# Two fused transformer blocks: another order around the two attentions, the out product and the last stores

## The reference, cut to what matters

```python
# block 1
xn = rmsnorm(x, norm_mix_g)
q_lat, kv_lat, k_rope, dq, dk, dv, gate_pre = split(xn @ w_in)
q, kv = rmsnorm(q_lat) @ mla_w_uq, rmsnorm(kv_lat) @ mla_w_ukv        # 8 heads, rope on 32 of 96 columns
o_mla = causal_attention(q_mla, k_mla, v_mla)
o1, o2 = causal_attention(dq[0], dk[0], dv), causal_attention(dq[1], dk[1], dv)   # 4 heads
o_diff = rmsnorm(o1 - lam * o2, diff_subln_g) * (1 - lambda_init)
g_mla, g_diff = split(sigmoid(gate_pre + b_gate))
merged = g_mla * (o_mla @ w_branch_mla) + g_diff * (o_diff @ w_branch_diff)
x = x + merged @ w_out
hn = rmsnorm(x, norm_ffn_g)
x = x + (silu(hn @ w_ffn_gate) * (hn @ w_ffn_up)) @ w_ffn_down
x = rmsnorm(x, norm_final_g)
# block 2
q, k, v, za, u, vs, zs, gm = split(rmsnorm(x, norm_g_2) @ w_in_2)
a = window_sink_attention(rope(q), rope(k), v, sinks)                 # 16 heads, keys of 128 + 64 tokens
a = (a * silu(za)) @ w_att_out
sgo = gelu(u) * (masked(w_s) @ layernorm(gelu(vs)) + b_s)
sgo = (sgo * silu(zs)) @ w_sg_out
ga, gs = split(sigmoid(gm + b_merge))
x = x + (ga * a + gs * sgo) @ w_o
return rmsnorm(x, final_g)
```

## Time and profile before

| | |
|---|---|
| median of 3 runs | 1262.26 us (1262.21 to 1262.78) |
| profiled execution | 1262.92 us, span 1261.2 us |
| TensorE's granted clock, mean | 0.999 |
| busy: PE | 1241.1 us, 98% |
| busy: DVE | 818.7 us, 65% |
| busy: ACT | 558.7 us, 44% |
| busy: POOL | 147.0 us, 12% |
| moved by DMA | 149.03 MB, mean 118 GB/s |

### The profile page before, as it was taken

How to read it: one execution, slowest core, us unless ns; L and a number is a source line. 1 busy time by engine, 2 the same in 40 slices (tenths; PEclk the granted TensorE clock), 3 DMA queues, 4 the chain that set the end, 5 groups by cost and what they waited for, 6 DMA issues and landing times.

```text
span 1261.2 us, 15542 instructions
## 1 busy us (share of the span) xinstructions
PE 1241.1 (98%) x6018; PEld 1039.8 (82%) x6018; DVE 818.7 (65%) x1272; ACT 558.7 (44%) x966; POOL 147.0 (12%) x208
## 2 busy tenths in 40 slices
PE   9999999999999999999999999999999999999997
PEld 8878888888878888888888888878888888888885
DVE  6885667754687555665665579858875436436687
ACT  5456564652455333333332263437763343223344
POOL 0001341231000100100000000005550000000200
PEclk9999999999999999999999999999999999999999
DMA  6242323129564943793332233321105322332971
GB/s 201 67 108 65 84 76 93 51 84 231 186 167 146 254 135 100 224 210 100 100 129 89 91 97 108 122 68 38 63 3 189 111 82 86 102 99 88 234 171 76
DMA packets 119077, 149.03 MB, mean 118 GB/s; under 512 B 14358, under 2 KB 90204, under 8 KB 119004
## 3 DMA queue, kind: packets, MB, share of 16 engines
q1 hardware_dynamic: 105436, 115.53, 28.8%
q0 software_dynamic: 13552, 32.51, 11.9%
q10 hardware_dynamic: 16, 0.00, 0.0%
HBM read 142.78 MB, written 2.10 MB: 115 GB/s over the span
## 4 chain that ended last, share of the span: by engine, by line
PE 86%; DVE 7%; ACT 3%; issue 2%; POOL 1%; DVEq 0%; ACTq 0%; POOLq 0%
PE ps_mm L2454 57%; PE ps_mm L2489 9%; PE ps_s L2757 3%; PE ps_mm L2757 3%; PE ps_t L2757 2%; PE ps_o L2757 2%; DVE w_lo L1513 1%; PE ps_s L2615 1%; ACT w_hi L908 1%; PE ps_o L2646 1%; PE ps_o L2902 1%; PE ps_mm L2529 1%; PE ps_s L2668 1%; PE ps_t L2626 1%; PE ps_o L2695 1%
## 5 line engine op out<-in xcount | busy, mean ns | idle before, releaser
L2454 PE MATMUL ps_mm<-act_hi,w_hi 128*128 128x512 f32 x944 | 372.2, 394 | 1.1 <-DVE w_lo L1513 1.1
L2454 PE MATMUL ps_mm<-act_hi,w_lo 128*128 128x512 f32 x944 | 370.0, 392 | 0.0
L2454 PE MATMUL ps_mm<-act_lo,w_hi 128*128 128x512 f32 x944 | 369.8, 392 | 0.0
L1513 DVE TENSOR_TENSOR w_lo<-stage,w_hi 128x2048 fp32r<-128x2048 f32 (+5 forms) x98 | 205.2, 2094 | 127.8 <-ACT w_hi L908 127.6
L908 ACT ACTIVATE w_hi<-stage 128x2048 fp32r<-128x2048 f32 (+5 forms) x99 | 171.9, 1736 | 143.1 <-PE ps_mm L2454 65.6
L2454 PEld LDWEIGHTS ps_mm<-act_hi,w_hi 128*128 128x128 f32 x944 | 177.4, 188 | 37.2 <-DVE w_lo L1513 2.4
L2454 PEld LDWEIGHTS ps_mm<-act_hi,w_lo 128*128 128x128 f32 x944 | 177.3, 188 | 35.6
L2454 PEld LDWEIGHTS ps_mm<-act_lo,w_hi 128*128 128x128 f32 x944 | 177.4, 188 | 34.7
L2489 PE MATMUL ps_mm<-w_hi,act_hi 128*128 128x512 f32 (+2 forms) x144 | 52.7, 366 | 0.6 <-DVE lat L1643 0.5
L2489 PE MATMUL ps_mm<-w_lo,act_hi 128*128 128x512 f32 (+2 forms) x144 | 52.2, 362 | 0.0
L2489 PE MATMUL ps_mm<-w_hi,act_lo 128*128 128x512 f32 (+2 forms) x144 | 52.2, 362 | 0.0
(11 more groups left out here) (518 smaller groups left out, 2363.4 us busy)
## 6 DMA issues: line engine op xcount, KB each, us to landing
stage<-in_w_in SPq DMA_DIRECT2D x43, 1024.0 KB, 5.3
sums<-in_w_ffn_down POOLq DMA_DIRECT2D x16, 1024.0 KB, 9.4
stage<-in_w_ffn_gate SPq DMA_DIRECT2D x11, 1024.0 KB, 7.6
stage<-in_w_ffn_up SPq DMA_DIRECT2D x11, 1024.0 KB, 7.0
stage<-in_w_ffn_down SPq DMA_DIRECT2D x8, 1024.0 KB, 5.0
osum<-in_w_out POOLq DMA_DIRECT2D x6, 1024.0 KB, 9.3
tsum<-in_w_o POOLq DMA_DIRECT2D x6, 1024.0 KB, 8.4
stage<-in_w_out SPq DMA_DIRECT2D x4, 1024.0 KB, 4.9
```

The source lines that it names most:

```text
L1513: V.tensor_tensor(w_lo[:, s, 0:k * w], raw, w_hi[:, s, 0:k * w].bitcast(F32), ALU.subtract).then_inc(w_lo_made, 1)
L2454: ins = T.matmul(ps_mm[:, 2 * bank_slot + m, :], wt[:, kk, m * P:(m + 1) * P], acts[ap][:, kk, :], start=(r == 0), stop=(r == per - 1), sk ...
```

## The change

In words: the first MLA scores are issued inside `mv` ahead of token block 3 (token order 0, 1, 2, 3); the squares of the last diff head move behind that step's gate banks and `hi`; in the merge ScalarE's sums come ahead of the gate banks and `hi` of the next unit between the two banks, VectorE's lo of the sums between the two gate products; in the stage of out the order of chunks, sums and units' lo changes (chunk 6's lo before chunk 5's) on both engines, and VectorE takes P6 out of its bank before P2; wg is turned one unit earlier, and VectorE's work on it, x3 and the sinks come before the last bank of za; `w_lo` in the window stream is made in quarters over four steps; the output is stored in eight halves.

```diff
@@ orders
+KEPT = {n: ("P6", "P2", "P7", "P5", "P4", "P3") if n == "out" else tuple(q for q in ORDER[n] if q != "P1") for n in GROUPED}
-    return 12 * GROUPED.index(n) + 2 * [q for q in ORDER[n] if q != "P1"].index(p)
+    return 12 * GROUPED.index(n) + 2 * KEPT[n].index(p)
+MERGED_LO = (0, 1, 2, 3, 4, 6, 5, 7)
@@ SP: stores
-            for pos, t in enumerate(FIN_ORDER[:3]):
-                sp.wait_ge(fin_made, pos + 1)
-                sp.wait_ge(fin_made_act, pos + 1)
-                sp.dma_start(ov[:, t, :], res[:, t, :]).then_inc(out_written, 16)
...
+            for half, t in ((0, 2), (1, 2), (1, 3), (0, 3), (0, 0), (1, 0), (0, 1), (1, 1)):
+                made = FIN_ORDER.index(t) + 1
+                sp.wait_ge(fin_made, made) if half else sp.wait_ge(fin_made_act, made)
+                cols = slice(512 * half, 512 * half + 512)
+                sp.dma_start(ov[:, t, cols], res[:, t, cols]).then_inc(out_written, 16)
@@ ScalarE: diff head, merge, out
-                if 0 <= hd < DH and r == 0:
+                if 0 <= hd < DH - 1 and r == 0:
...
                 for u in DIFF_STREAM.started(p):
                     hi(u + 1)
+                if hd == DH - 1 and r == 0:
+                    for t in range(TT):
+                        act.wait_ge(o_copied, 4 * hd + t + 1)
+                        squares(o_sb[:, t * P:(t + 1) * P], o_sq[:, t * P:(t + 1) * P], diff_ssq[:, t:t + 1], o_squared)
...
             for i in range(1, 4):
                 hi(GATE_B[i] + 1)
-                for m in range(2):
-                    gate_bank(GATE_B[i], m, 8 + 2 * i + m)
-                hi(MRG_D[i - 1] + 1)
                 if i > 1:
                     merged_sums_hi(i - 2)
+                gate_bank(GATE_B[i], 0, 8 + 2 * i)
+                if i < 3:
+                    hi(MRG_D[i - 1] + 1)
+                gate_bank(GATE_B[i], 1, 8 + 2 * i + 1)
                 if i < 3:
                     for m in range(2):
                         merge_hi(2 * i - 2 + m)
+                else:
+                    hi(MRG_D[i - 1] + 1)
+            merge_hi(4)
             hi(uo)
-            merge_hi(4)
             merge_hi(5)
+            merged_sums_hi(2)
+            hi(uo + 1)
             merge_hi(6)
-            hi(uo + 1)
             merge_hi(7)
-            merged_sums_hi(2)
@@ VectorE: quarters, merge, out
+            def lo_quarter(u, h):
...
+                n = k * w // 4
+                ins = V.tensor_tensor(w_lo[:, s, h * n:(h + 1) * n], stage[:, s, h * n:(h + 1) * n],
+                                      w_hi[:, s, h * n:(h + 1) * n].bitcast(F32), ALU.subtract)
+                if h == 3:
+                    ins.then_inc(w_lo_made, 1)
...
                 lo(GATE_B[i] + 1)
-                for m in range(2):
-                    gate_norm(GATE_B[i], m, 8 + 2 * i + m)
-                lo(MRG_D[i - 1] + 1)
+                gate_norm(GATE_B[i], 0, 8 + 2 * i)
                 if i > 1:
                     merged_sums_lo(i - 2)
+                gate_norm(GATE_B[i], 1, 8 + 2 * i + 1)
+                lo(MRG_D[i - 1] + 1)
...
             merge(4)
             merge(5)
+            merge_lo(4)
+            merged_sums(2)
             lo(uo)
-            merge_lo(4)
-            merge_lo(5)
             merge(6)
-            merged_sums(2)
             merge(7)
             merge_lo(6)
             lo(uo + 1)
+            merge_lo(5)
             merge_lo(7)
             merged_sums(3)
             lo(uo + 2)
             merged_sums_lo(2)
             merged_sums_lo(3)
+            lo(uo + 3)
             dve.wait_ge(res_landed, 16 * TT)
+            keep_product("out", "P6")
             keep_product("out", "P2")
-            lo(uo + 3)
-            keep_product("out", "P6")
@@ VectorE: za, window steps
-                for m in range(2):
-                    normed(gz[:, 2 * i + m, :], u, m)
+                normed(gz[:, 2 * i, :], u, 0)
                 if i < 3:
+                    normed(gz[:, 2 * i + 1, :], u, 1)
...
                     V.memset(wg_t[CHUNK:P, :, 0:CHUNK], 0.0).then_inc(v2_wg_made, 1)
+                    dve.wait_ge(consts_landed, 80)
+                    after(link(V.tensor_scalar(nsinkb, sinkb, -1.0, None, ALU.mult)))
+                    normed(gz[:, 2 * i + 1, :], u, 1)
...
-                for h in range(2):
+                for h in range(4):
                     for u in WIN_STREAM.started(p - 3 - h):
-                        lo_half(u + 1, h)
+                        lo_quarter(u + 1, h)
@@ TensorE: MLA start, out, wg
-            wide_unit(U0["mv"], lat_kv)
-            pe.wait_ge(bank_free, freed(U0["mv"] - 1, 1))
-            pe.wait_ge(kpe_spread, MH)
+            def first_scores(t):
+                if t == 2:
+                    pe.wait_ge(bank_free, freed(U0["mv"] - 1, 1))
+                    pe.wait_ge(kpe_spread, MH)
+                    mla_scores(0)
+            wide_unit(U0["mv"], lat_kv, token_done=first_scores)
...
-                            pe.wait_ge(chunk_lo_made, (MERGED_AT if n == "out" else Y_AT) + 2 * kk + (1 if p == "P1" else 2))
+                            pe.wait_ge(chunk_lo_made, (MERGED_AT + MERGED_LO.index(2 * kk + (p == "P2")) if n == "out" else Y_AT + 2 * kk + (p == "P2")) + 1)
...
                 straight(U0["za"] + i, "F", acts_x)
-                if i == 3:
+                if i == 2:
                     pe.wait_ge(wg_landed, 16)
```

More of the change, by code:

```diff
@@ L718, in _ @@
             ov = A["out"].rearrange("a (t p) d -> p (a t) d", p=P)
-            for pos, t in enumerate(FIN_ORDER[:3]):
-                sp.wait_ge(fin_made, pos + 1)
-                sp.wait_ge(fin_made_act, pos + 1)
-                sp.dma_start(ov[:, t, :], res[:, t, :]).then_inc(out_written, 16)
[L723 to L728, removed]
+            for half, t in ((0, 2), (1, 2), (1, 3), (0, 3), (0, 0), (1, 0), (0, 1), (1, 1)):
[3 more added lines that the diff above has]
+                sp.dma_start(ov[:, t, cols], res[:, t, cols]).then_inc(out_written, 16)
+            sp.wait_ge(out_written, 16 * 2 * TT)
         def landed_count(u):
@@ L1514, in lo @@
                                 ).then_inc(w_lo_made, 1)
+            def lo_quarter(u, h):
+                s = u % 2
+                src, k, w = unit_source(u)
+                dve.wait_ge(w_hi_made, u + 1)
+                n = k * w // 4
[3 more added lines that the diff above has]
+                    ins.then_inc(w_lo_made, 1)
             def lo_half(u, h):
@@ L1903, in merged_sums_lo @@
                 dve.wait_ge(op_hi_made, i + 1)
-                dve.wait_ge(chunk_lo_made, MERGED_AT + 2 * i + 2)
+                dve.wait_ge(chunk_lo_made, MERGED_AT + max(MERGED_LO.index(2 * i), MERGED_LO.index(2 * i + 1)) + 1)
                 V.scalar_tensor_tensor(out=sm_lo[:, i, :, :].rearrange("p a n -> p (a n)"),
@@ L2177, in _ @@
                     V.memset(wg_t[CHUNK:P, :, 0:CHUNK], 0.0).then_inc(v2_wg_made, 1)
+                    dve.wait_ge(consts_landed, 80)
+                    after(link(V.tensor_scalar(nsinkb, sinkb, -1.0, None, ALU.mult)))
+                    normed(gz[:, 2 * i + 1, :], u, 1)
             NP = WIN_PIECES
-            dve.wait_ge(consts_landed, 80)
-            after(link(V.tensor_scalar(nsinkb, sinkb, -1.0, None, ALU.mult)))
             for p in range(WIN_STEPS + 2):
@@ L2600, in _, with mla_scores @@
                 straight(U0["kn"] + i, "F", lat_kv)
-            wide_unit(U0["mv"], lat_kv)
-            pe.wait_ge(bank_free, freed(U0["mv"] - 1, 1))
-            pe.wait_ge(kpe_spread, MH)
+            def mla_scores(p):
+                h = p // 3
+                if p >= 2:
+                    pe.wait_ge(exp_made, mla_done(p - 2))
+                if p % 3 == 0:
+                    pe.wait_ge(q_spread, h + 1)
+                for k, t, cc in mla_tiles(p):
+                    T.matmul(ps_s[:, p % 2, cc], qm[0:MQ, h, t * P:(t + 1) * P], km[0:MQ, h, 0:P * (t + 1)],
+                             start=True, stop=False)
+                    ins = T.matmul(ps_s[:, p % 2, cc.stop - P:cc.stop], ident_r[:, :], causal_r[:, :],
+                                   start=False, stop=True)
+                ins.then_inc(s_full, 1)
+            def first_scores(t):
[4 more added lines that the diff above has]
+            wide_unit(U0["mv"], lat_kv, token_done=first_scores)
             NP = MLA_PIECES
             for p in range(MLA_STEPS):
[L2608 to L2619, removed]
+                if 1 <= p < NP:
+                    mla_scores(p)
                 q = p - LAG
```

## The result

The changed kernel took 1255.12 us (median of 4, 1254.83 to 1255.48) against 1262.31 for the kernel before in the same job: ratio 0.9941, 95% interval 0.9928 to 0.9953. The forecast was 1255.3, its range 1253.2 to 1259.2. The profiled execution took 1255.48 against 1262.92 before, 7.44 shorter, with a span of 1253.7.

A forecast was written before the change was run, and what follows sets the result against it. TensorE was taken to set the end nearly everywhere, so gains come from its waits, the start or the tail. Eight terms sum to 6.95 us: 1262.92 becomes 1255.97 profiled, 1255.3 for the median; range 1253.2 to 1259.2.

The forecast's parts named there:

- GATE_B[1]: Last diff head, squares behind the next hi: VectorE's lo can start at 277.23 instead of 277.51, gain 0.28 us.
- MLA scores: Step 0's scores ahead of the last token's values: maximum, exp and third scores come earlier, gain 0.85 us.
- GATE_B[2] and [3]: Merge, hi ahead of the second gate bank: a wait of 0.40 us goes at each of two units, gain 0.80.
- the ramps: At waits that vanish whole: the longer first matmul after each is saved too, 0.4 us as a separate term.
- Out product: New order around it: 2.33 us of waits go, a new wait of 0.72 plus 0.16 comes before P1; gain 1.45.
- the other side of the range: Out product's lower bound: -0.72 us if the new wait before P1 comes and the old ones stay.
- The first rival: Out and window stages: waits come back one step later, gain only 4.35 us, so 1257.9; chance 0.20.
- Window, first scores: Start of window attention: maximum earlier, exp table load comes on the path, third scores 1.30 us earlier.
- Quarters: w_lo in the window stream: three pt_lo waits behind halves go (1.12 us), with short ones; gain taken as 1.15.
- The rival in which VectorE becomes the bound: Window attention: each quarter's 0.61 us passes on to TensorE, 4.0 slower in all, 1266.3; chance 0.05.
- Half stores: Tail: a quarter of a megabyte leaves earlier, gain 0.72 us; bounds 1.4 and -1.3.
- GpSimd and VectorE: Rival, window stream: quarters held by GpSimd's gate products once per unit, gain only 0.64 us, 1261.6; chance 0.08.

The follow-up runs named there:

- e1: Changed kernel with the first MLA scores behind all four token blocks of mv again: 1256.28 us.
- e2: Changed kernel with the old order in the merge only (next unit's hi behind both gate banks, lo of the sums behind the next unit's lo): 1256.98 us.
- e3: Changed kernel with the old order around the out product only (chunks 0 to 7 in order, lo(uo) ahead of the sums, P2 kept before P6): 1256.85 us.
- e4: Changed kernel with w_lo in the window stream in halves over two steps again: 1257.61 us.
- e5: Changed kernel with wg turned after the last unit of za again and VectorE's x3, wg copies, memset and sink constants behind both its banks: 1256.17 us.
- e6: Changed kernel with the old stores again (three blocks whole, the last in halves): 1255.74 us.
- e11: Kernel before with one part alone, w_lo of the window stream in quarters over four steps: 1260.71 us beside 1262.74, ratio 0.9985.
- e8: Changed kernel with VectorE's lo of out's first unit ahead of the merged chunks' sums, and ScalarE's hi of the second unit ahead of its sums: 1255.76 us.
- e10: Changed kernel with lo of out's first unit right behind chunk 4's rest, P6's sums behind chunk 7's rest, ScalarE's sums moved likewise: 1255.74 us.
- e7: Changed kernel with GpSimd's product of zs one step later, right behind the scaling of the probabilities: 1254.30 us.

## Why the prediction was right

The mechanism held at each place: TensorE sets the end, each part aimed at one of its waits, and e1 to e6 and e11 give the parts back at their own places with no later wait that takes them. Two exceptions: e2's part showed at P1 as well, and the 0.26 at GATE_B[1] rests on the comparison of the two traces alone, since no run undid the squares. The place where a new wait was named is the place where it came (P1, 0.53 idle for 0.72).

*MLA scores, GATE_B[1].* 0.87 and 0.26 for 0.85 and 0.28. The rows that VectorE and ScalarE already had gave these to a few hundredths, since what ends last next could be dated.

*GATE_B[2] and [3].* 1.13 for 0.80 with 0.22 of the ramps, which were a term of their own. The rest of about 0.1 is within what two such waits' own 0.16 were guessed at. That this order also pays at P1 (0.53 in e2) stands in the prediction only as "VectorE has the 1.22 out of the way".

*Out product.* -0.78 and 2.37 for -0.88 and 2.33. e8 and e10 show that the other side of the range was near: with the order a little different P1's wait is paid inside. The first rival, in which waits come back later, is what happened in this stage to both further steps tried.

*Window, first scores.* 1.12 for 1.30; the wait left is 0.23 as forecast. ScalarE's silu ended at 841.88, where the forecast's 845.45 less the 3.73 gained by then is 841.72; this is nearly all of the 0.18. The table load now stands on the path:

```profile
841.25 0.63 ACT L1335 ACTIVATE gz<-gz 128x512 f32<-128x512 f32 x1 [4.88 <-DVE gz L2154]
841.90 1.28 ACT L1358 ACT_TABLE_LOAD   x1
```

*Quarters.* The one term that was mis-sized: 1.95 for 1.15. The three waits behind halves gave 1.0 of it, where 1.12 was worked out. The other 0.95 lies in five steps whose transposes or values began 0.15 to 0.31 late behind an idle time of 0 to 0.07; the prediction said that they "go with them" and gave them 0.03. A matmul's record covers its neighbour's start by 0.16, so a delay up to that leaves no idle time in the view of the waits. The rival in which VectorE becomes the bound is refuted by e4 and e11: sixteen operations of 0.69 instead of eight of 1.23 made nothing late.

```profile
L1529 DVE TENSOR_TENSOR w_lo<-stage,w_hi 128x512 fp32r<-128x512 f32 x16 | 11.1, 693 | 0.0
```

*Half stores.* 0.59 by the two traces and the same by e6, for 0.72. Smaller transfers did not cost speed here (385 GB/s from 1251 to 1252, 381 from 1258 to 1260 before), so the sentence of the Trainium skill (Perfetto Trace Analysis, DMA Optimizations) on larger ones did not bind; the one on splitting so that some start sooner did.

*GpSimd and VectorE.* The rival's mechanism is real and was there before the change, but the quarters did not meet it: their mean stayed at 0.69. It held the min twice in the window stretch (1.20 and 1.10 after, 1.23 and 1.09 before), which e7 took away, together with the other effect told there.

**What it comes to.** The sum was 6.95 and 7.44 came: 0.8 more from the quarters, less 0.18 at the window's start, 0.13 at the tail and 0.11 at the start of the run; the other places, the 0.4 of ramps among them, make up the last 0.1. That the total is nearer than its worst term is luck: the misses had different signs.

## What to carry to other kernels

Where one engine is busy all the time, date what would end last next at each of its waits, and price a wait by the shift of start times, not by idle time alone: short delays hide inside overlapping records. Cutting an operation that stands in a tight loop into smaller pieces over more steps pays where each step has a little slack. When new orders of one engine's list only move a wait, as two did at P1, ask next what work can leave that engine; no run here tried that.

## What the runs showed of the hardware that was not expected

The hold of the earlier trace rows met long operations of VectorE with two operands from on-chip memory too: the unit's w_lo behind the window stream took 3.27 instead of 2.29 beside GpSimd's two-operand product. Changed kernel, VectorE and GpSimd:

```profile
942.78 3.27 DVE L1520 TENSOR_TENSOR w_lo<-stage,w_hi 128x2048 fp32r<-128x2048 f32 x1 [2.50 <-ACT w_hi L908]
...
942.61 1.29 POOL L863 TENSOR_TENSOR gu<-tmp,gu 128x512 f32<-128x512 f32 x1
```

Two operands on VectorE's side are not needed for it: in the MLA attention a one-operand scaling of 512 columns took 1.32 beside such a product, and 0.49 where none ran. Changed kernel:

```profile
172.81 1.28 POOL L786 TENSOR_TENSOR dq<-dq,tmp 128x512 f32<-128x512 f32 x1
...
173.05 1.32 DVE L1796 TENSOR_SCALAR prob<-prob,small 128x512 f32<-128x512 f32 x1
```

Beside GpSimd's one-operand scaling VectorE's two-operand operations were not held to its end: a quarter of w_lo kept its 0.68, and the scaling its 0.93; over all runs the longest beside a scaling were 0.78 for a quarter and 0.36 for a min. Changed kernel:

```profile
908.35 0.93 POOL L857 TENSOR_SCALAR prob<-prob,small 128x256 f32<-128x256 f32 x1
...
908.75 0.68 DVE L1529 TENSOR_TENSOR w_lo<-stage,w_hi 128x512 fp32r<-128x512 f32 x1
```

The Trainium skill (SBUF — State Buffer, Who interferes with whom) has a VectorE operation with two such inputs contend with any GpSimd instruction that reads there. These rows agree for the two-operand product and not for the one-operand scaling.
